# Dealing out 160 modulation sums anew over VectorE's stretches, and taking the first norm's reciprocal ahead of the first weight parts

## What is computed

```python
c_act = jax.nn.silu(c)                                   # c is (1, 1024)
for l in range(DEPTH_2):                                 # 2
    mod = (c_act @ w_ada[l] + b_ada[l]).reshape(bsz, 3, 3, D_MODEL)
    ...                                                  # used in every norm of layer l
kv_mod = (c_act @ w_ada_kv + b_ada_kv).reshape(bsz, 2, D_MODEL)

def _rms_norm(x, gain):                                  # the first norm of all, on x
    y = xf * lax.rsqrt(jnp.mean(xf * xf, axis=-1, keepdims=True) + EPS)
```

## Time and profile before

| | |
|---|---|
| median of three executions | 3862.42 us |
| profiled execution, device time | 3863.18 us |
| profiled execution, span of the trace | 3861.4 us |
| busy: TensorE matmuls, VectorE, ScalarE | 94%, 50%, 37% of the span |
| stage w_in, from the first product to its end | 27.2 to 161.5 us |
| stage w_out ends, first block's feed-forward net | 580.4 us, 801 to 1187 us |

### The profile page before, as it was taken

The page is one execution under the profiler, slowest core; times in us unless marked ns, Lnnn a source line. Parts: engine busy times, 40 slices in busy tenths (PEclk is TensorE's granted clock), DMA queues, the critical chain, the costliest instruction groups (busy, mean ns, idle before and its releaser), DMA issues.

```text
span 3861.4 us, 50061 instructions
## 1 busy us (share of the span) xinstructions
PE 3639.3 (94%) x19328; PEld 2940.1 (76%) x19328; DVE 1916.9 (50%) x3873; ACT 1421.8 (37%) x2510; POOL 107.3 (3%) x183
## 2 busy tenths in 40 slices
PE   7779999989998999999999989999899998889999
PEld 6669956778877888777777768888788886668887
DVE  6756735566776333454555544333433345764332
ACT  3251212432223222455555643223322233863222
POOL 0000001011111000000000000000000000000000
PEclk9889999989998999999999999999999999999999
DMA  6200026236772232211111112232222221012222
GB/s 239 93 1 1 1 85 231 99 128 243 283 239 105 81 116 76 72 67 60 50 50 50 72 53 88 87 109 98 89 82 93 88 79 44 2 41 73 91 102 77
DMA packets 47160, 360.82 MB, mean 93 GB/s; under 512 B 5217, under 2 KB 5601, under 8 KB 28129
## 3 DMA queue, kind: packets, MB, share of 16 engines
q1 hardware_dynamic: 23472, 270.36, 19.3%
q0 software_dynamic: 23472, 87.50, 6.5%
HBM read 355.74 MB, written 2.10 MB: 93 GB/s over the span
## 4 chain that ended last, share of the span: by engine, by line
PE 83%; DVE 8%; issue 4%; ACT 3%; DVEq 1%; DMA 1%; PEld 0%; ACTq 0%; PEldq 0%; POOL 0%; SPq 0%; POOLq 0%
PE bank L797 21%; PE bank L802 21%; PE bank L803 21%; PE bank L1615 5%; PE bank L759 2%; PE bank L1949 1%; PE bank L1937 1%; PE bank L1966 1%; PE bank L2417 1%; DVE w_lo_sb L1219 1%; PE bank L2384 1%; PE bank L1925 1%; PE bank L777 1%; PE bank L726 1%; PE bank L2406 1%
## 5 line engine op out<-in xcount | busy, mean ns | idle before, releaser
L797 PE MATMUL bank<-x_hi_sb,w_hi_sb 128*128 128x512 f32 x2888 | 1156.7, 401 | 61.6 <-DVE w_lo_sb L1219 19.3
L803 PE MATMUL bank<-x_hi_sb,w_lo_sb 128*128 128x512 f32 x2888 | 1134.0, 393 | 0.0
L802 PE MATMUL bank<-x_lo_sb,w_hi_sb 128*128 128x512 f32 x2888 | 1133.9, 393 | 0.0
L797 PEld LDWEIGHTS bank<-x_hi_sb,w_hi_sb 128*128 128x128 f32 x2888 | 547.4, 190 | 211.9 <-issue 71.2
L1042 ACT ACTIVATE w_hi_sb<-slab_sb 128x1024 fp32r<-128x1024 f32 (+2 forms) x549 | 500.9, 936 | 508.3 <-PE bank L797 319.6
L1219 DVE TENSOR_TENSOR w_lo_sb<-slab_sb,w_hi_sb 128x1024 fp32r<-128x1024 f32 (+2 forms) x549 | 573.4, 1076 | 185.2 <-ACT w_hi_sb L1042 168.7
L803 PEld LDWEIGHTS bank<-x_hi_sb,w_lo_sb 128*128 128x128 f32 x2888 | 546.9, 189 | 117.7
L802 PEld LDWEIGHTS bank<-x_lo_sb,w_hi_sb 128*128 128x128 f32 x2888 | 548.1, 190 | 107.8
L1385 DVE TENSOR_TENSOR hid_sb<-silu_gate_sb,bank 128x512 f32<-128x512 f32 x110 | 75.6, 687 | 593.5 <-PE bank L803 593.2
L797 PE MATMUL bank<-hid_hi_sb,w_hi_sb 128*128 128x512 f32 x880 | 344.0, 391 | 2.6 <-DVE w_lo_sb L1219 2.6
L803 PE MATMUL bank<-hid_hi_sb,w_lo_sb 128*128 128x512 f32 x880 | 343.6, 390 | 0.0
(11 more groups left out here) (349 smaller groups left out, 3776.8 us busy)
## 6 DMA issues: line engine op xcount, KB each, us to landing
slab_sb<-weights SPq DMA_DIRECT2D x80, 2048.0 KB, 7.7
keep_sb<-ada POOLq DMA_DIRECT2D x133, 512.0 KB, 5.0
slab_sb<-weights SPq DMA_DIRECT2D x44, 1536.0 KB, 6.4
slab_sb<-weights SPq DMA_DIRECT2D x20, 1280.0 KB, 5.8
tables_sb<-ada POOLq DMA_DIRECT2D x14, 512.0 KB, 6.1
work_sb<-ada POOLq DMA_DIRECT2D x13, 512.0 KB, 7.8
h_sb<-x SPq DMA_DIRECT2D x4, 512.0 KB, 6.5
out<-h_sb SPq DMA_DIRECT2D x8, 256.0 KB, 2.5
```

The source lines that it names most:

```text
L797: mm = pe.matmul(out, w_hi[p][:, w], hi, start=first, stop=False)
L802: pe.matmul(out, w_hi[p][:, w], lo, start=False, stop=False)
L803: return pe.matmul(out, w_lo[p][:, w], hi, start=False, stop=last)
```

## The change

Five things are done.

1. `ADA_TURNS` becomes (29, 47, 84): turn 0 has 9 pieces more, turn 1 has 12 more, turn 2 has 21 fewer. The rings stay as they are.
2. Behind the last weight part of w_in VectorE does 17 pieces in a row, not 8.
3. In w_out it does 5 before each of the sums k = 3 to 6, not 2.
4. In the feed-forward net it does none behind the first pair of hidden tiles; 3 behind each pair of the second half, not 4; 2 behind each output tile of the first half, not 3.
5. At the start the root (ScalarE) and the reciprocal (VectorE) come ahead of the first four weight parts.

```diff
-ADA_TURNS = (20, 35, 105)
+ADA_TURNS = (29, 47, 84)
...
                     dve.tensor_tensor(hid_lo[:, at + pair, :], hid[:, pair, :], hid_hi[:, at + pair, :].bitcast(F32),
                                       ALU.subtract).then_inc(hid_lo_ready, 1)
-                    if aside is not None:
+                    if aside is not None and (which, pair) != ("first", 0):
                         aside(half, which)
...
                 act_sum_square(e, k, h[:, k, :])
+            act_sums_root(e, False)
             for q in range(PARTS):
                 act_w_hi(e, q, D)
-            act_sums_root(e, False)
...
                 dve_sum_square(e, k)
+            dve_sums_done(e)
+            e.sc.pos += 1
             for q in range(PARTS):
                 dve_w_lo(e, q, D)
-            dve_sums_done(e)
-            e.sc.pos += 1
             dve_scale_split(e, V("g_mix_pre"))
...
             for q in (2, 3):
                 dve_w_lo(e, q, D)
-            dve_ada(e, 8)
+            dve_ada(e, 17)
...
             for k in range(3, KT - 1):
-                dve_ada(e, 2)
+                dve_ada(e, 5)
                 dve_sum_square(e, k)
...
                 if at in ("first", "mid", "last"):
-                    dve_ada(e, 4 if half else 3)
+                    dve_ada(e, 3)
                 elif half == 0 or at < 5:
-                    dve_ada(e, 1 if half else 3)
+                    dve_ada(e, 1 if half else 2)
```

## The result

The changed kernel took 3883.88 us (median of four executions, 3880.09 to 3886.09) against 3863.76 for the kernel before, a ratio of 1.0053 with a 95% interval of 1.0041 to 1.0065: slower by 0.5%, clear of the 0.2% that the prediction named as what a measurement can tell, and 4 us above its 3880 us. The medians differ by 20.1 us, the profiled executions by 16.9 (3880.09 against 3863.18 us of device time), where the sum had +17.2.

A forecast was written before the change was run, and what follows sets the result against it. TensorE was taken to bound the kernel (83% of the span), VectorE 8%, with added pieces costing where VectorE is waited for. +12.7 + 21.7 - 17.2 = +17.2 on 3862.4 gave 3880 us, range 3868 to 3889.

The forecast's parts named there:

- The sum: Whole kernel: +12.7 + 21.7 - 17.2 = +17.2 us on the profiled execution, giving 3880 us.
- Part 1: Start: root and reciprocal sooner let the scaling start 1.8 us sooner; -1.5 us taken, ends -0.9 and -1.8.
- Part 2: End of w_in: nine more pieces wait on the ring's loads; +12.7 us including the start, ends +6.6 and +18.
- Part 3: w_out: twelve more pieces where VectorE is already last, their loads sharing bandwidth with a slab; +21.7 us, low end 13.7.
- Part 4: Feed-forward net: 21 fewer pieces remove 10.7 us of TensorE's waits and 6.5 us at low clock; -17.2 us, low end -10.7.
- the three large terms: w_in with the start +12.7 us, w_out +21.7 us, feed-forward net -17.2 us.
- The rival of a smaller gain: Net: a third piece still late or the clock falls all the same; -10.7 instead of -17.2, 3886 us; 10%.
- Loads that keep up: w_in and w_out: rings deliver as fast as VectorE works, only its own time counts; +3, 3866 us; 8%.
- Loads slower still: w_in and w_out: loads lie closer than anywhere in the trace; +18 + 25 - 15 = +28, 3890 us; 12%.
- Faster: TensorE, not VectorE, last at both stage ends, so added pieces are free; 3844 us, or 3857 if w_out pays; 3%.
- What was to show it: Profile signs: w_in's load waits and end near 174, TensorE's wait near L945, first product near 25.4, one short net wait.

The follow-up runs named there:

- the kernel with the free places: Kernel before, with 13 sums fewer in the net, placed ahead of w_in's first weight part, behind w_out's norm and in w_cq: 3845.43 us, ratio 0.9959.
- the run without loads: Changed kernel with every sum, but without the loads of w_in's last 17 pieces and 15 of w_out's 20: 3863.11 us, ratio 0.9996.
- half rows: Changed kernel with the loads of w_in's last 17 sums and 15 of w_out's 20 bringing 256 KB instead of 512 KB: 3876.22 us, ratio 1.0031.

## Why the prediction was right, and where it was not

**The sum** was +17.2 against +16.9, and that it fits to 0.3 us is luck. Parts 1 and 2 were 4.0 us too low; part 3 was 1.6 too high and missed 1.0 behind it; part 4 was 0.6 short. What brought the sum back are 3.0 us in three stretches whose code did not change (-1.3, -0.3 and -1.4 in the table), for which no cause is known. The direction and the three large terms are not luck: w_in's and w_out's went where their edits were undone, and the net's stands alone in the kernel with the free places.

**Part 1, the start, failed.** The step was "If they stay there until the same moment as before, half of the gain is lost", with -1.5 taken, and -0.9 as the low end. The first product came 1.0 us sooner, not 1.8: TensorE's column sums began 0.5 us later in this execution (13.4 against 12.9), and most of the rest is that. And the clock did not rise at the same moment, but 1.6 us later (first short product at 31.82, not 30.23), so nothing was left (+0.2 at the last weight part; no change in the run with the opening alone). I had looked at when TensorE started and not at what it did before: the new order puts its spreading (L969) at 17.5 instead of 22.25 and opens 6.5 us of idle time ahead of the first product, where 2.9 had been.

**Part 2, w_in, had the mechanism and was mis-sized.** Parts 1 and 2 were to give +12.7 and gave +16.7, inside the ends of +6.6 and +18. Of the 4.0 us missing, 1.5 are part 1's. The rest is the size of the loads, taken as 4.1 us, a mean of the two seen: from issue to use, one of the eight that VectorE waited for took 3.7 us and seven 4.6 to 4.9. The first turn began at 155.84 and not 155.05 (0.8 us), three turns took 17.75 us for 17.1 (0.7), and the last piece, which the sum had right behind the one before, waited 1.32 us for its own load, until 176.15; the four copies took 0.3 us less. In the two other traces with this code the end of w_in cost 15.9 and 14.5 us, not 16.5. The low end was wrong in kind: I set VectorE's own time behind the 158.45 at which the eight sums had ended, waits included. Counted from the last weight part, 17 sums take 19.5 us and end at 158.8, ahead of TensorE. With loads on time the term would have been nothing, as the run without loads shows.

**Part 3, w_out, right in size.** +21.7 was forecast, +20.1 measured (+19.9 and +22.0 in two other traces with the same code there), and 1.0 more behind it because TensorE came back at 1.2 GHz, which I had not counted: from L945 to L1320 are 60.7 to 62.2 us in the five traces with the long wait, and 59.7 to 59.9 in the six others. Of the 20.1, 13.8 are VectorE's sums (13.7 forecast). The engines moved a little more than taken, 400 and 412 GB/s where I had put 363. But the sum had the bytes alone set the last landing, and by that half rows would have removed the other 6.3 us; 1.7 came back. The longest waits there are for single loads issued next to the slab, which take 7 to 11 us, with half a row too. What makes them that long stays open.

The Trainium skill, "DMA: Bandwidth & Descriptors", table "Specifications", has 358 GB/s for a core, half of what it gives a stack of memory that two cores share. Both windows exceed it, in a kernel that runs on one core.

**Part 4, the net, right.** -17.2 forecast, -17.8 measured: the waits went from 11.5 to 0.9 us (10.7 forecast), and the one left stands behind the opening slab, 0.94 us for 0.85. The granted clock over this stretch went from 0.97 to 0.99, worth some 8 us by an estimate from these rounded figures, so the clock fits as the rest. The rival of a smaller gain falls, also in five other kernels that have 325.6 or 325.7 us from L1265 to the first L3022, and 326.5 in the run without loads; the three traces with the old net have 340.2, 341.8 and 342.8.

**The rivals.** Loads that keep up: the run without loads, 3863 us, is what they would give, against the 3866 worked out. Loads slower still: w_in came near that end, w_out did not (and the -15 in that rival's sum has no row behind it). Faster: its condition, a load every 1.2 us in w_in, would indeed have made w_in free, but not w_out.

**What was to show it.** TensorE's wait ahead of L945 was 21.6 us for some 20, and one wait under 1 us in the net for one; VectorE waited nine times for loads, not six to eight, at the end of w_in, and the stage ended at 178, not 174; the first product was at 26.1, not 25.4. The pieces in w_out did not start 1.15 us apart throughout, which would have spoken for loads that keep up.

## What to carry to other kernels

Work that is to be put in the shadow of another engine needs its data there too: count the engine's time from the moment at which it is free, and the ring's time for a turn (use, issue, load) beside it, and take the longer; in w_in the first cost nothing and the second 16.5 us. A place is free if the trace shows the engine idle there for something else: 13.4 us of idling took six sums for nothing that the trace shows, while w_out, where the engine was already waited for, charged the full length of each. And when a step moves sooner, look at how long the engine behind it now idles before it starts, since that can cost as much in clock as the step gives.

## What the runs showed that I had not expected

**How long TensorE stays at 1.2 GHz behind an idle stretch differs from run to run.** With 6.5 us of idling ahead of the first product, the stretch from the first product to the first short one lasted 5.7, 5.6, 5.2, 4.4, 6.1, 4.3 and once 3.1 us in seven traces whose code is the same up to there. With 2.5 to 2.9 us of idling it was 3.0 and 3.1 us, and once 3.5, with 0.7 us 0.3. So the new opening lost its gain in most executions, not in all: the one with 3.1 us, that of the run without loads, had its last weight part at 137.8, 1.2 us sooner than before. What chooses the length stays open.

**The same code differs by 2 us between L1841 and L2994** with the granted clock from 515 to 535 us: 48.2 us at 0.92, 50.2 at 0.78 and 0.79. (The changed kernel reaches this code 15 us later, so that window is another stretch there.) A single pair of profiles cannot tell 2 us in this kernel without a look at the clock of each stretch.

**The rate of the DMA engines near full share is not one figure.** With 512 KB loads and one slab in flight they moved 400 and 412 GB/s in the two windows of the changed kernel, more than the 363 GB/s of the earlier trace rows; but in the run with w_in's sums back to 8 it was 347 GB/s from 592 to 600 us, at a share of 0.97, with such loads alone.

**A piece loaded next to a slab takes about twice as long.** In the changed kernel the loads at the end of w_in, with no slab beside them, could be used 3.7 to 4.9 us behind their issue, and one of w_out ahead of the slab 5.6 (587.92 to 593.55). Those issued within about 1 us of a slab took 10.1 us there, 10.6 with w_in's sums back to 8 (580.29 to 590.90), and 7.3 and 9.4 with half rows.
